# Splitting 576 tokens as 384 and 192 instead of 288 and 288 in the projections, with five matmuls per weight tile

## What is computed

```python
def diff_attn_project(h, w_in):
    proj = h @ w_in                      # (tokens, 2048) @ (2048, 8192): q, k, v, gate
...
def diff_attn_output(o, g, subln_w, w_out):
    of = head_rms_norm(o.astype(jnp.float32)) * subln_w.astype(jnp.float32) * (1.0 - LAMBDA_INIT)
    gated = of.reshape(b, s, DA_WIDTH).astype(g.dtype) * jax.nn.silu(g)
    return gated @ w_out                 # (tokens, 2048) @ (2048, 2048)
...
def ret_project(h, w_in, pos):
    proj = h @ w_in                      # (tokens, 2048) @ (2048, 12288): q, k, v, gate
...
def ret_output(o, g, w_out):
    return (on.astype(g.dtype) * jax.nn.silu(g)) @ w_out     # (tokens, 4096) @ (4096, 2048)
```

## Time and profile before

| | before |
|---|---|
| median of 3 runs | 3670.21 us (3666.57 to 3674.71) |
| profiled execution | 3668.89 us |
| its span | 3667.1 us |
| TensorE busy | 3510.0 us, 96% |
| VectorE busy | 1678.3 us, 46% |
| ScalarE busy | 983.8 us, 27% |
| mean granted TensorE clock | 0.982 of full |

### The profile page before, as it was taken

The page is one execution under the profiler, slowest core; times in us unless marked ns, Lnnn a source line. Parts: engine busy times, 40 slices in busy tenths (PEclk is TensorE's granted clock), DMA queues, the critical chain, the costliest instruction groups (busy, mean ns, idle before and its releaser), DMA issues.

```text
span 3667.1 us, 69262 instructions
## 1 busy us (share of the span) xinstructions
PE 3510.0 (96%) x28260; PEld 3166.3 (86%) x28260; DVE 1678.3 (46%) x2681; ACT 983.8 (27%) x1552; POOL 150.7 (4%) x87
## 2 busy tenths in 40 slices
PE   7999999999999989788999999999999999999998
PEld 7987887888788878578999999989999999989998
DVE  4466565656565665336324242423242424333345
ACT  4222222222222232214322222222222222332123
POOL 1000001100200020022000000000000000000000
PEclk9999999999999989889999999999999999999999
DMA  5476987889698969643434243434343434443333
GB/s 180 147 221 208 285 263 236 251 264 295 208 283 261 287 218 305 184 160 129 145 96 158 92 152 102 145 100 140 108 142 109 133 118 130 164 134 107 107 127 121
DMA packets 472191, 642.86 MB, mean 175 GB/s; under 512 B 35649, under 2 KB 294850, under 8 KB 468738
## 3 DMA queue, kind: packets, MB, share of 16 engines
q1 hardware_dynamic: 407122, 565.91, 49.1%
q10 hardware_dynamic: 64336, 72.24, 5.9%
q0 software_dynamic: 416, 0.28, 0.1%
HBM read 566.09 MB, written 70.65 MB: 174 GB/s over the span
## 4 chain that ended last, share of the span: by engine, by line
PE 53%; DVE 1%; issue 1%; DMA 1%; ACT 1%; POOL 1%; SPq 0%; ACTq 0%; DVEq 0%; POOLq 0%
PE low_banks L986 45%; PE high_banks L986 6%; PE high_banks L989 1%; DMA area<-in_cache_v 1%; POOL area L1951 1%; DVE WL L1539 0%; SPq L931 0%; ACT WH L1259 0%; DVE area L1836 0%; DMA WR<-in_w_in_ret 0%; ACT XH L1259 0%; DVE area L1561 0%; ACT area L1259 0%; POOL area L1991 0%; DVE area L1886 0%
## 5 line engine op out<-in xcount | busy, mean ns | idle before, releaser
L986 PE MATMUL low_banks<-XH,WH 128*128 128x288 f32 (+2 forms) x6656 | 1546.7, 310 | 44.8 <-DVE XL L1544 20.9
L986 PE MATMUL low_banks<-XH,WL 128*128 128x288 f32 (+2 forms) x6656 | 1460.6, 297 | 0.0
L986 PE MATMUL low_banks<-XL,WH 128*128 128x288 f32 (+2 forms) x6656 | 1458.2, 297 | 0.0
L986 PEld LDWEIGHTS low_banks<-XH,WH 128*128 128x128 f32 x6656 | 1089.0, 191 | 170.0 <-issue 119.7
L986 PEld LDWEIGHTS low_banks<-XL,WH 128*128 128x128 f32 x6656 | 1090.1, 190 | 0.0
L986 PEld LDWEIGHTS low_banks<-XH,WL 128*128 128x128 f32 x6656 | 1088.8, 190 | 0.0
L1539 DVE TENSOR_TENSOR WL<-WR,WH 128x1024 fp32r<-128x1024 f32 x436 | 531.4, 1219 | 791.0 <-ACT WH L1259 785.8
L1259 ACT ACTIVATE WH<-WR 128x1024 fp32r<-128x1024 f32 x436 | 461.7, 1059 | 1197.4 <-PE low_banks L986 879.2
L986 PE MATMUL high_banks<-area 128*32 128x128 f32 (+6 forms) x6768 | 646.6, 377 | 37.1 <-DMA area<-in_cache_v 14.2
L986 PEld LDWEIGHTS high_banks<-area 128*32 128x32 f32 (+2 forms) x6768 | 321.8, 130 | 243.7 <-issue 213.7
L1635 DVE STREAM_TRANSPOSE area<-area 128x512 f32<-128x512 f32 x512 | 343.2, 699 | 215.0 <-DMA area<-in_cache_k 171.5
(11 more groups left out here) (120 smaller groups left out, 919.8 us busy)
## 6 DMA issues: line engine op xcount, KB each, us to landing
area<-in_cache_k SPq DMA_DIRECT2D x512, 256.0 KB, 5.8
area<-in_cache_v SPq DMA_DIRECT2D x512, 256.0 KB, 5.0
WR<-in_w_in_ret SPq DMA_DIRECT2D x200, 512.0 KB, 3.6
WR<-in_w_in_attn SPq DMA_DIRECT2D x136, 512.0 KB, 6.0
out<-area ACTq DMA_DIRECT2D x73, 512.0 KB, 3.1
WR<-in_w_out_ret SPq DMA_DIRECT2D x68, 512.0 KB, 3.4
area<-in_state_ret SPq DMA_DIRECT2D x64, 512.0 KB, 5.6
WR<-in_w_out_attn SPq DMA_DIRECT2D x32, 512.0 KB, 5.7
```

The costliest lines, as they stand in the source:

```text
L986: return nc.tensor.matmul(out, a, b, start=start, stop=stop, skip_group_check=True)
```

## The change

The tokens of a two-piece weight tile are split as 0 to 383 ("wide") and 384 to 575 ("rest", 192 tokens). XH and XL become two halves of one SBUF tensor `XX`, so that one matmul can read the 192 rest tokens of XH and of XL as 2 x 192 = 384 moving columns. It leaves WH·XH in columns 0 to 191 of the rest bank and WH·XL in columns 192 to 383; WL·XH of the rest tokens is added to columns 0 to 191 by a matmul of 192 columns. A weight tile has five matmuls, of 384, 384, 384, 384 and 192 columns. The two halves of the rest bank are added on draining: ScalarE copies columns 0 to 191 out (`rest_copied`), then drains the wide bank; VectorE adds columns 192 to 383 to what ScalarE wrote. For q, k, v and y that addition counts in `proj{cb}_drained`; for the gates ScalarE waits for it (`rest_summed`) and applies Silu to the sum in SBUF. For "+" VectorE makes three additions instead of two. One-piece tiles are as before.

```diff
-HALF = T // 2
+WIDE = 384
+REST = T - WIDE
+GATES = ("g", "gr")
...
     if k == "evacuate":
-        return {f"proj{a['cb']}_drained": 1}
+        if len(a["pieces"]) < 2 or a["kind"] == "+":
+            return {f"proj{a['cb']}_drained": 1}
+        if a["kind"] in GATES:
+            return {"rest_copied": 1, "rest_summed": 1, f"proj{a['cb']}_drained": 1}
+        return {"rest_copied": 1, f"proj{a['cb']}_drained": 2}
...
-        pieces = ((0, 0, HALF), (1, HALF, T)) if span is None else (span,)
+        pieces = ((0, 0, WIDE), (1, WIDE, T)) if span is None else (span,)
...
-        XH, XL = sb("XH", [128, KT, T], f32r), sb("XL", [128, KT, T], f32r)
+        XX = sb("XX", [128, 2, KT, T], f32r)
+        XH, XL = XX[:, 0, :, :], XX[:, 1, :, :]
...
                 w = slice(cb * 128, cb * 128 + 128)
+                if len(pieces) == 2:
+                    wide, rest = bank[2 * cb][:, 0:WIDE], bank[2 * cb + 1]
+                    high, low = WH[:, slot, k, w], WL[:, slot, k, w]
+                    mm(wide, high, XH[:, kt, 0:WIDE], start=start, stop=False)
+                    mm(wide, high, XL[:, kt, 0:WIDE], start=False, stop=False)
+                    mm(rest[:, 0:2 * REST], high, XX[:, :, kt, WIDE:T], start=start, stop=False)
+                    mm(wide, low, XH[:, kt, 0:WIDE], start=False, stop=stop)
+                    last = mm(rest[:, 0:REST], low, XH[:, kt, WIDE:T], start=False, stop=stop)
+                    if full:
+                        last.then_inc(sem[full], 1)
+                    return
...
-                for n, (b, lo, hi) in enumerate(pieces):
-                    if n:
-                        o.link(last)
-                    last = nc.scalar.activation(dst[:, lo:hi], bank[2 * cb + b][:, 0:hi - lo], f)
-                if extra is not None:
+                copy(dst[:, WIDE:T], bank[2 * cb + 1][:, 0:REST]).then_inc(sem["rest_copied"], 1)
+                last = nc.scalar.activation(dst[:, 0:WIDE], bank[2 * cb][:, 0:WIDE], f)
+                if not gate:
+                    last.then_inc(sem[f"proj{cb}_drained"], 1)
+                    return
+                o.link(last)
+                act.wait_ge(sem["rest_summed"], c.done("rest_summed"))
+                last = nc.scalar.activation(dst[:, WIDE:T], dst[:, WIDE:T], f)
+                if kind == "g":
                     o.link(last)
-                    last = copy(extra, dst[:, SEQ:T])
+                    last = copy(sgN[:, hh * 2 + cb, :], dst[:, SEQ:T])
                 last.then_inc(sem[f"proj{cb}_drained"], 1)
...
+                full = "w_used" if cb else "proj0_full"
+                rest = bank[2 * cb + 1]
+                if kind != "+" and len(pieces) == 2:
+                    mine = target(kind, hh)[:, cb, WIDE:T]
+                    name = "rest_summed" if kind in GATES else f"proj{cb}_drained"
+                    dve.wait_ge(sem["rest_copied"], c.done("rest_copied"))
+                    v.tensor_tensor(mine, rest[:, REST:2 * REST], mine, ADD).then_inc(sem[name], 1)
...
+                    if len(pieces) == 2:
+                        o.link(last)
+                        last = v.tensor_tensor(dst[:, WIDE:T], rest[:, REST:2 * REST], dst[:, WIDE:T], ADD)
```

More of the change, by code:

```diff
@@ L880, in hybrid_step_kernel, with target @@
         DVE_NAMES = [n for n in sem_names if n not in PE_NAMES + SP_NAMES + ACT_NAMES + POOL_NAMES]
+        def target(kind, hh):
+            if kind in "qk":
+                return (qT if kind == "q" else kT)[hh]
+            if kind in ("gr", "y"):
+                return (rsg if kind == "gr" else yT)[:, 2 * hh:2 * hh + 2, :]
+            return {"v": vT, "g": sg, "qr": raw[0], "kr": raw[1], "vr": rvT}[kind]
         block = ctx.enter_context(nc.Block())
@@ L1290, in evacuate @@
                 act.wait_ge(sem[f"proj{cb}_drained"], c.before(f"proj{cb}_drained"))
-                f, extra = ACT.Copy, None
+                gate = kind in GATES
+                dst, f = target(kind, hh)[:, cb, :], ACT.Silu if gate else ACT.Copy
                 if kind == "g":
@@ L1294, in evacuate @@
                     act.wait_ge(sem["carried"], c.before("carried"))
-                    dst, f, extra = sg[:, cb, :], ACT.Silu, sgN[:, hh * 2 + cb, :]
                 elif kind == "gr":
@@ L1298, in evacuate @@
                         act.wait_ge(sem[n], c.before(n))
-                    dst, f = rsg[:, hh * 2 + cb, :], ACT.Silu
                 elif kind in ("q", "k"):
@@ L1303, in evacuate @@
                     act.wait_ge(sem["full5"], c.before("full5"))
-                    dst = (qT if kind == "q" else kT)[hh][:, cb, :]
                 elif kind == "v":
@@ L1307, in evacuate @@
                     act.wait_ge(sem["full5"], c.before("full5"))
-                    dst = vT[:, cb, :]
                 elif kind in ("qr", "kr"):
                     act.wait_ge(sem["rotated"], c.before("rotated"))
-                    dst = raw[kind == "kr"][:, cb, :]
                 elif kind == "vr":
                     act.wait_ge(sem["full7"], c.before("full7"))
-                    dst = rvT[:, cb, :]
                 else:
@@ L1317, in evacuate @@
                         act.wait_ge(sem[n], c.before(n))
-                    dst = yT[:, hh * 2 + cb, :]
-                for n, (b, lo, hi) in enumerate(pieces):
-                    if n:
-                        o.link(last)
-                    last = nc.scalar.activation(dst[:, lo:hi], bank[2 * cb + b][:, 0:hi - lo], f)
-                if extra is not None:
+                if len(pieces) < 2:
+                    b, lo, hi = pieces[0]
+                    nc.scalar.activation(dst[:, lo:hi], bank[2 * cb + b][:, 0:hi - lo], f).then_inc(sem[f"proj{cb}_drained"], 1)
+                    act.wait_ge(sem[f"proj{cb}_drained"], c.done(f"proj{cb}_drained"))
+                    return
[3 more added lines that the diff above has]
+                    last.then_inc(sem[f"proj{cb}_drained"], 1)
+                    return
+                o.link(last)
+                act.wait_ge(sem["rest_summed"], c.done("rest_summed"))
+                last = nc.scalar.activation(dst[:, WIDE:T], dst[:, WIDE:T], f)
+                if kind == "g":
                     o.link(last)
-                    last = copy(extra, dst[:, SEQ:T])
+                    last = copy(sgN[:, hh * 2 + cb, :], dst[:, SEQ:T])
                 last.then_inc(sem[f"proj{cb}_drained"], 1)
@@ L1552, in evacuate @@
             def evacuate(g, cb, kind, hh, pieces, layer=None):
+                full = "w_used" if cb else "proj0_full"
[5 more added lines that the diff above has]
+                    v.tensor_tensor(mine, rest[:, REST:2 * REST], mine, ADD).then_inc(sem[name], 1)
                 if kind == "+":
-                    full = "w_used" if cb else "proj0_full"
                     dve.wait_ge(sem[full], c.before(full))
```

## The result

The changed kernel takes 3689.94 us (median of 6 runs, 3685.02 to 3695.82) against 3670.16 for the kernel before (6 runs): ratio 1.0053, 95% interval 1.004 to 1.0066. That is 19.8 us or 0.5% slower; the forecast was 3686. The profiled execution took 3693.6 us, its span is 3691.8.

A forecast was written before the change was run, and what follows sets the result against it. TensorE, busy 96% of the span, was taken as the bound. The profiled 3668.9 us plus 6.7 for TensorE's tiles and 10 for waits on VectorE's additions gave 3686 us, range 3655 to 3718.

The forecast's parts named there:

- What bounds it: Whole kernel: TensorE is busy 96% of the span, so time added or taken there is span, nearly one for one.
- The line of fixed price and columns: TensorE matmuls: each costs a fixed 13.3 ns and 0.417 ns per column, so 384 columns take 173.3 ns.
- The load as the floor of a short matmul: Two-piece tiles: the next weight load holds the 192-column matmul to 110 ns, not 93; tile 3.3 ns dearer, +9.7 us.
- late loads: In 228 of 3168 tiles the next load isn't issued early; there 13.3 ns are saved, −3.0 us in all.
- Two runs of columns: Third matmul reading XH and XL far apart: taken as 0, possibly 7.6 ns each, up to 24 us.
- The drains: Two-piece tiles' drains: VectorE's additions mostly hidden, TensorE waiting where VectorE is late; +10 us, bounds 3 and 20.
- The three places: TensorE waits at the drain of q (0.7 us), drain of k (1.1) and first gate (0.85), recurring: 8.8 us.
- the gates' 3.4 us: After gate drains, VectorE's late addition, Silu and token copy delay TensorE 0.85 us, four times.
- The fast one: Rival: the 192-column matmul costs only its stream, a 93.3 ns step; −42 us on tiles, total 3637; chance 0.14.
- That of 120 ns: Rival: the fixed 13.3 ns come on top of the load, 192 columns take 120 ns; total 3715; chance 0.17.
- VectorE did not become the bound: Rival on the attention: 64 two-piece drains hold VectorE in lockstep with TensorE, +54 us instead of 10; 3730; chance 0.09.
- The sign that I named for the fast rival: In a pure stretch of the changed trace, the start after the 192-column matmul 93 ns behind it, against 108 to 113.

The follow-up runs named there:

- 64-column kernel: The changed kernel with the last matmul of a two-piece tile cut from 192 to 64 columns: 3681.48 us, ratio 1.0032.

## Why the prediction was right, point by point

- **What bounds it.** Right: TensorE's gain or loss of time is span. One short matmul per tile, 7 ns dearer, shows in a kernel of 3.7 ms.
- **The line of fixed price and columns.** Right for 384 columns on the whole (173 to 175 ns for the forecast 173.3) and for 320 and 256 with six matmuls (800.0 ns measured and forecast). It failed at 512 columns and a little behind them, which the forecast did not use.
- **The load as the floor of a short matmul.** Right: the floor is shown by itself with 64 columns, that the load is what sets it is read from the earlier trace rows. Taken as 110 ns, measured as 113.3 in the output projection (285 ns for the pair, or 111.7, in the medians). So the tile rose by 6.7 ns and not 3.3: 2940 times 6.7, less the 3 us of the late loads, is some +17 us instead of +6.7. That value was inside the bounds (113 ns), and the term of the sum was undersized by 10 us. The Trainium skill, page "TensorE: Matmul & The Clock Gate", section "LDWEIGHTS (loading the stationary operand)", has a load of 128 columns at 106.7 ns, with no term for the moving width. The 64-column kernel agrees that the moving width doesn't enter, and the step measured here is 5 to 7 ns longer.
- **Late loads.** Right in kind: the 64-column kernel gained 8.5 us where the 228 tiles explain 12. A count through the trace of before shows which ends these are. Where the next load has weights of 128x32, 64x128 or 32x128 it comes late, 177 times out of 177; before a load of 128x128 weights it does so 42 times out of 2943, and 9 times out of 48 before one of 128x64.
- **Two runs of columns.** Taken as free, and shown to be free, in a row of 512.
- **The drains.** The three places were right, in place and kind, and the waits too: 12.6 us of them in the list, of which 2.6 replace waits for ScalarE's copy in the same list of before (`PE high_banks L989 <- ACT area L1322: 2.6, 4, 0.8`). Forecast: 8.8 by places, 10 in all. But their worth in time is less: two kernels without those of `natural` and `scores` gained 8 us by the medians (3689.9 to 3682.3, 3660.3 to 3652.1) and 5 and 7 by the ratios, whose intervals overlap in both pairs. So this term was oversized by some 2 to 5 us. The lists of waits show where it went wrong: the gates' 3.4 us were counted as added, but they stand in for waits of 5.0 us for VectorE's scaling of the prompt output, which is why all waits rose by only 7.3 us (148.6 to 155.9). These are sums of one profiled execution each.
- **The sum.** 17 and 5 to 8 us make 22 to 25, where 19.8 (15 to 24 by the interval) was measured and 16.7 forecast. With the 7.3 us of the lists it is 24, the upper end of the interval. That the total came within 4 us is in part luck: one term was 10 us too small, the other too large. (The upper end of the forecast's own range, 3668.9 + 15.5 + 20, is 3704 and not 3703.)
- **The rivals.** The fast one is refuted by the 64 columns. The 81 ns that the same page of the Trainium skill has for a sustained pair of load and matmul of 128 columns ("Back-to-back issue gap") do not appear with these weights: matmuls of 64 columns still cost the tile 113.3 ns. That of 120 ns lies outside 113.3 (and 256 columns with no load in the way stay at 120). VectorE did not become the bound: without its additions 13 us remain.
- **What would show it.** The sign that I named for the fast rival, a start 93 ns or less behind the short matmul, did appear (88 ns), and it meant nothing: the next step was longer by as much. The sign should have been the sum over the pair or the tile.

## What to carry to other kernels

Fewer matmuls for the same columns save only a small fixed price each, and a matmul shorter than the weight load behind it gives that back and more. Before splitting, find from the trace how close two loads of the same size can stand, and keep every matmul longer than that (here 256 columns were, 192 were not). A helper engine's new instruction costs its place in that engine's list, not its length: look for who waits for it, whether that one waits for more than it reads, and whether the new wait only stands in for one that came behind it. A wait for "the latest drain" was the cheaper thing to mend here, and it was worth as much as dropping the additions.

## What I had not expected of the hardware

- The matmul behind a short one has its start recorded 88 ns after it at 192 columns and 30 ns after at 64, and then lasts until the load allows: the pair takes 285 and 283 ns. Recorded starts around a short matmul are not issue prices.
- A tile's time at full clock came out even over 60 tiles: 806.7 ns with 192 or 64 columns, 800.0 with six matmuls of 320 and 256, 793.3 with five of 320, 512 and 256.
- A matmul of 512 columns with its own weight load steps 231 ns, whether its columns are adjacent or in two runs.
- Silu's table load, 1.28 us, stood ahead of ScalarE's wait for the bank when Silu was the drain's first instruction (207.57 to 208.85 in the trace of before, for a drain at 209.41); with a plain copy put first it moved between copy and Silu, into the drain (212.01 above). VectorE was later still, so it cost nothing here.
